# Input layer norm of a streaming encoder layer: mean, centring, then squares, with half 1 centred between half 0's chunks

## What is computed

```python
def _layer_norm(x, g, b):
    xf = x.astype(jnp.float32)
    mu = jnp.mean(xf, axis=-1, keepdims=True)
    var = jnp.mean(jnp.square(xf - mu), axis=-1, keepdims=True)
    return ((xf - mu) * lax.rsqrt(var + LN_EPS) * g + b).astype(x.dtype)

hp = _layer_norm(jnp.concatenate([meta_rows, x_prompt], axis=1), ln_in_g, ln_in_b)
hs = _layer_norm(x_sample, ln_in_g, ln_in_b)
z = h @ w_in + b_in           # u, q, k, v and two gates, 1024 -> 4096
...                           # pooling mixer, stick-breaking attention, out projection, norm, MLP, norm
```

## Time and profile before

| | |
|---|---|
| median of 3 runs | 827.62 us (827.31 to 828.57) |
| the profiled execution, its own time | 829.96 us |
| its span | 828.2 us |
| mean granted TensorE clock | 0.988 |
| PE busy | 798.3 us, 96% of the span |
| DVE, ACT, POOL busy | 504.2, 390.8, 113.8 us |
| chain that ended last | PE 93%, DVE 5%, ACT 1% |
| HBM traffic | 71 MB, mean 85 GB/s |

### The profile page before, as it was taken

The page is one execution under the profiler, slowest core; times in us unless marked ns, Lnnn a source line. Parts: engine busy times, 40 slices in busy tenths (PEclk is TensorE's granted clock), DMA queues, the critical chain, the costliest instruction groups (busy, mean ns, idle before and its releaser), DMA issues.

```text
span 828.2 us, 14458 instructions
## 1 busy us (share of the span) xinstructions
PE 798.3 (96%) x5859; PEld 766.6 (93%) x5859; DVE 504.2 (61%) x844; ACT 390.8 (47%) x653; POOL 113.8 (14%) x134
## 2 busy tenths in 40 slices
PE   4899999999999999999999999999999999999994
PEld 2789879998988899999999999999999999999994
DVE  6753434546454456885868678774767877445454
ACT  4542425655555465563546664333554433344333
POOL 5230000190000000006550000000000000000452
PEclk9799999999999999999999999999999999999997
DMA  9503222112111202234111214222221422222202
GB/s 352 200 28 135 77 96 75 56 39 80 53 51 51 75 28 77 78 103 151 51 53 52 70 57 153 77 103 77 77 70 57 154 77 102 77 77 84 70 29 86
DMA packets 23082, 71.62 MB, mean 86 GB/s; under 512 B 2464, under 2 KB 6704, under 8 KB 22640
## 3 DMA queue, kind: packets, MB, share of 16 engines
q1 hardware_dynamic: 22192, 67.97, 24.5%
q0 software_dynamic: 544, 2.52, 0.9%
q10 hardware_dynamic: 288, 0.33, 0.1%
HBM read 65.96 MB, written 4.85 MB: 85 GB/s over the span
## 4 chain that ended last, share of the span: by engine, by line
PE 93%; DVE 5%; ACT 1%; DMA 0%; issue 0%; POOL 0%; ACTq 0%; DVEq 0%
PE lin L582 14%; PE lin L583 14%; PE lin L584 14%; PE z L1018 5%; PE z L1021 5%; PE z L1020 5%; PE lin L923 3%; PE lin L924 3%; PE lin L925 3%; PE z L797 3%; PE lin L1064 2%; PE lin L1063 2%; PE lin L1062 2%; PE z L783 1%; PE z L855 1%; PE z L584 1%
## 5 line engine op out<-in xcount | busy, mean ns | idle before, releaser
L582 PE MATMUL lin<-h_hi,whi 128*128 128x288 f32 (+1 forms) x832 | 247.2, 297 | 0.0
L583 PE MATMUL lin<-h_lo,whi 128*128 128x288 f32 (+1 forms) x832 | 245.9, 296 | 0.0
L584 PE MATMUL lin<-h_hi,wlo 128*128 128x288 f32 (+1 forms) x832 | 245.0, 294 | 0.0
L584 PEld LDWEIGHTS lin<-h_hi,wlo 128*128 128x128 f32 x832 | 156.6, 188 | 0.0
L582 PEld LDWEIGHTS lin<-h_hi,whi 128*128 128x128 f32 x832 | 156.5, 188 | 0.1
L583 PEld LDWEIGHTS lin<-h_lo,whi 128*128 128x128 f32 x832 | 156.4, 188 | 0.1
L1706 DVE TENSOR_TENSOR wlo<-raw,whi 128x1024 fp32r<-128x1024 f32 x65 | 80.9, 1245 | 34.9 <-ACT whi L1095 29.8
L1095 ACT ACTIVATE whi<-raw 128x1024 fp32r<-128x1024 f32 x58 | 60.9, 1051 | 51.1 <-PE lin L584 32.8
L1512 ACT ACTIVATE relu_t<-lin,vecs 128x288 f32<-128x288 f32 x60 | 30.0, 500 | 91.5 <-PE lin L584 88.1
L2133 DVE TENSOR_TENSOR relu_sq<-relu_t 128x288 f32<-128x288 f32 x60 | 27.5, 458 | 64.7 <-ACT relu_t L1512 64.7
L1018 PE MATMUL z<-f_ops,whi 128*128 128x288 f32 x216 | 64.2, 297 | 0.7 <-issue 0.7
(11 more groups left out here) (332 smaller groups left out, 1908.9 us busy)
## 6 DMA issues: line engine op xcount, KB each, us to landing
raw<-w_stream SPq DMA_DIRECT2D x88, 512.0 KB, 3.5
w_set<-w_sets SPq DMA_DIRECT2D x32, 384.0 KB, 3.6
r<-x_t SPq DMA_DIRECT2D x8, 296.0 KB, 5.6
y<-r SPq DMA_DIRECT2D x16, 144.0 KB, 1.9
kcache<-k_cache SPq DMA_DIRECT2D x1, 2048.0 KB, 13.9
vcache<-v_cache SPq DMA_DIRECT2D x1, 2048.0 KB, 10.5
k_new<-k_t POOLq DMA_DIRECT2D x1, 1184.0 KB, 4.8
v_new<-v_t POOLq DMA_DIRECT2D x1, 1024.0 KB, 5.7
```

Of the source, the lines that this page charges most:

```text
L582: pe.matmul(out, w_h, hi, start=first, stop=False)
L583: pe.matmul(out, w_h, lo, start=False, stop=False)
L584: return pe.matmul(out, w_l, hi, start=False, stop=last)
```

## The change

The norm takes another order. Of half 0, DVE adds the raw chunks by pairs and PE sums them: the mean comes first, with no shift. DVE centres six chunks and POOL two (BY_DVE0 = (6, 8)), ACT squares six of the centred chunks and DVE two, whose sum is added, and PE sums the seven squares. The variance stays in its PSUM bank: ACT's Ln reads it there, with epsilon as bias, and DVE's Newton step starts from it there.

Of half 1, PE sums the eight raw chunks directly as the mean, ahead of the keys. Its chunks are centred on DVE between half 0's scale and low part, squared on ACT between half 0's high parts, and summed by PE between the chunks of the first pair of key units (`between`).

PE begins with 14 products of the constant matrix by itself (WARM), 128 columns each, into a bank that nobody reads. The low part of key unit 0 goes from POOL to DVE. On SP, units 0 and 1 go ahead of x's half 1, units (1,0) and (1,1) ahead of `bv` and the key cache, the value cache behind units (1,2) and (1,3), and `wpool` last, from ACT's queue. POOL makes its mask constants directly after unit 1's low part, and waits for half 1's Ln before it fills `mask_new`, whose place holds epsilon until then.

The diff, cut to its core:

```diff
-        BY_DVE0 = (5, 4)
+        BY_DVE0 = (6, 8)
+        SQ_ACT0 = (0, 1, 2, 6, 3, 4)
+        SQ_DVE0 = (5, 7)
+        WARM = 14
...
-            for j in range(RAW):
-                load_unit(0, j, first=True)
+                for j in range(2 * h, 2 * h + 2):
+                    load_unit(0, j, first=True)
+            load_unit(1, 0)
+            load_unit(1, 1)
             sp.dma_start(bv[:, :], bv_d).then_inc(bv_in, 16)
             sp.dma_start(kcache[:, :, :], kc_d).then_inc(kc_in, 16)
-            load_unit(1, 0)
-            load_unit(1, 1)
-            sp.dma_start(vcache[:, :, :], vc_d).then_inc(vc_in, 16)
             load_unit(1, 2)
             load_unit(1, 3)
+            sp.dma_start(vcache[:, :, :], vc_d).then_inc(vc_in, 16)
+            sp.dma_start(wpool[:, :, :], wpool_d).then_inc(wpool_in, 16)
...
-            def x_shift(h):
-                pe.wait_ge(x_in[h][0], 16)
-                pe.matmul(r0_shift(h), ones_f[:, :], r0[:, 0, half0(h)], start=True, stop=True).then_inc(n0_shift, 1)
-            def pair_sums(h, p):
-                c, start, stop = half0(h), p == 0, p == KC // 2 - 1
-                pe.wait_ge(pair_added, h * (KC // 2) + p + 1)
-                pe.matmul(r0_mean(h), inv_d[:, :], pair0[:, p, c], start=start, stop=stop)
-                pe.wait_ge(pair_sq_added, h * (KC // 2) + p + 1)
-                pe.matmul(r0_sq(h), inv_d[:, :], sq0[:, sq0_slot(2 * p), c], start=start, stop=stop)\
-                    .then_inc(n0_terms, 1)
-            pe.wait_ge(made, 2)
-            x_shift(0)
-            pair_sums(0, 0)
-            x_shift(1)
-            for p in range(1, KC // 2):
-                pair_sums(0, p)
+            def warm():
+                pe.matmul(lin[:, 1, 0:P], inv_d[:, :], inv_d[:, :], start=True, stop=True)
+            def square_sum(h, slot, first, last):
+                op = pe.matmul(r0_sq(h), inv_d[:, :], sq0[:, slot, half0(h)], start=first, stop=last)
+                if last:
+                    op.then_inc(n0_terms, 1)
+            pe.wait_ge(made, 1)
+            for _ in range(WARM):
+                warm()
+            for p in range(KC // 2):
+                pe.wait_ge(pair_added, p + 1)
+                op = pe.matmul(r0_mean(0), inv_d[:, :], pair0[:, p, :], start=p == 0, stop=p == KC // 2 - 1)
+            op.then_inc(n0_summed, 1)
+            for n, k in enumerate(SQ_ACT0):
+                pe.wait_ge(n0_sq, n + 1)
+                square_sum(0, k, n == 0, False)
+            pe.wait_ge(n0_sq_v, 3)
+            square_sum(0, SQ_DVE0[0], False, True)
+            for k in range(KC):
+                pe.wait_ge(x_in[1][k // 2], 16)
+                op = pe.matmul(r0_mean(1), inv_d[:, :], r0[:, k, half0(1)], start=k == 0, stop=k == KC - 1)
+            op.then_inc(n0_summed, 1)
...
+                    if between is not None and 1 <= k <= KC:
+                        between(k - 1)
+            def square_sum1(k):
+                pe.wait_ge(n0_sq, len(SQ_ACT0) + k + 1)
+                square_sum(1, k, k == 0, k == KC - 1)
+            keys_pair(0, 0, square_sum1)
...
-                act.wait_ge(n0_d, KC * h + k + 1)
-                if k >= 6:
-                    act.wait_ge(n0_terms, h * (KC // 2) + 1)
-                elif h and k < 2:
-                    act.wait_ge(n0_terms, KC // 2)
-                nc.scalar.activation(sq0[:, sq0_slot(k), half0(h)], r0[:, k, half0(h)], ACT.Square).then_inc(n0_sq, 1)
-            def mean0_out(h):
-                act.wait_ge(n0_terms, (h + 1) * (KC // 2))
-                nc.scalar.activation(var0[:, half0(h)], r0_mean(h), ACT.Square).then_inc(n0_msq, 1)
-                nc.scalar.activation(mean0[:, half0(h)], r0_mean(h), ACT.Copy).then_inc(n0_mean, 1)
+                centred0(k, h)
+                nc.scalar.activation(sq0[:, k, half0(h)], r0[:, k, half0(h)], ACT.Square).then_inc(n0_sq, 1)
...
-                act.wait_ge(n0_var, 2 * h + 2)
-                nc.scalar.activation(rstd0[:, c], var0[:, c], ACT.Ln).then_inc(n0_guess, 1)
+                act.wait_ge(n0_terms, h + 1)
+                nc.scalar.activation(rstd0[:, c], r0_sq(h), ACT.Ln, bias=eps0[:, :]).then_inc(n0_guess, 1)
...
+            act.wait_ge(n0_summed, 1)
+            nc.scalar.activation(mean0[:, :], r0_mean(0), ACT.Copy).then_inc(n0_mean, 1)
+            for k in SQ_ACT0:
                 square0(k, 0)
             split_keys(0)
             split_keys(1)
+            act.wait_ge(made, 2)
             root0(0)
             act.wait_ge(vecs_in, 16)
             norm0_hi(0, 0)
+            for k in range(1, KC):
+                norm0_hi(k, 0)
+                square0(k - 1, 1)
+                if k in (4, 6):
+                    split_keys(k // 2)
+            square0(7, 1)
...
+            def add_pair(p):
+                dve.wait_ge(x_in[0][p], 16)
+                tt(pair0[:, p, :], r0[:, 2 * p, half0(0)], r0[:, 2 * p + 1, half0(0)], ALU.add).then_inc(pair_added, 1)
+            def centre0(k, h):
                 if k == 0:
+                    dve.wait_ge(n0_summed, h + 1)
+                if k == 0 and h == 0:
+                    dve.wait_ge(n0_mean, 1)
+                tt(r0[:, k, half0(h)], r0[:, k, half0(h)], r0_mean(h), ALU.subtract).then_inc(n0_centred_v, 1)
+            def squares_0():
+                a, b = SQ_DVE0
+                dve.wait_ge(n0_centred_v, BY_DVE0[0])
+                tt(sq0[:, a, half0(0)], r0[:, a, half0(0)], r0[:, a, half0(0)], ALU.mult).then_inc(n0_sq_v, 1)
+                dve.wait_ge(n0_centred_g, KC - BY_DVE0[0])
+                tt(sq0[:, b, half0(0)], r0[:, b, half0(0)], r0[:, b, half0(0)], ALU.mult).then_inc(n0_sq_v, 1)
+                dve.wait_ge(n0_sq_v, 2)
+                tt(sq0[:, a, half0(0)], sq0[:, a, half0(0)], sq0[:, b, half0(0)], ALU.add).then_inc(n0_sq_v, 1)
             def inverse0(h):
+                c, out = half0(h), r0_rstd(h)
+                dve.wait_ge(n0_guess, 3 * h + 1)
+                nc.vector.tensor_scalar(out, r0_sq(h), LN_EPS, -0.5, ALU.add, ALU.mult).then_inc(n0_rstd, 1)
                 dve.wait_ge(n0_guess, 3 * h + 3)
+                dve.wait_ge(n0_rstd, 3 * h + 1)
+                tt(out, out, guess0[:, c], ALU.mult).then_inc(n0_rstd, 1)
+                dve.wait_ge(n0_rstd, 3 * h + 2)
+                stt(out=out, in0=out, scalar=1.5, in1=rstd0[:, c], op0=ALU.add, op1=ALU.mult).then_inc(n0_rstd, 1)
+                dve.wait_ge(n0_rstd, 3 * h + 3)
...
+                dve.wait_ge(*square_taken0(k, h))
...
+                add_pair(p)
+            for k in range(BY_DVE0[0]):
+                centre0(k, 0)
+            squares_0()
+            split_keys(0)
             inverse0(0)
             dve.wait_ge(vecs_in, 16)
             scale0(0, 0)
+            for k in range(1, KC):
                 scale0(k, 0)
+                centre0(k - 1, 1)
+                norm0_lo(k - 1, 0)
+            centre0(7, 1)
...
+            pool.wait_ge(n0_mean, 1)
+            for k in range(BY_DVE0[0], KC):
+                nc.gpsimd.tensor_tensor(r0[:, k, half0(0)], r0[:, k, half0(0)], mean0[:, :], ALU.subtract)\
+                    .then_inc(n0_centred_g, 1)
+            pool.wait_ge(lo_split, 1)
             lo_part(1)
...
+            pool.wait_ge(n0_guess, 4)
             nc.gpsimd.memset(mask_new[:, :, :], 0.0).then_inc(win_done, 1)
```

More of the change, by code:

```diff
@@ L709, in keys_pair @@
                         last = keys_half(m0 + 1, h, k - LAG)
-                last.then_inc(done, 1)
-            keys_pair(0, 0)
-            for p in range(KC // 2):
-                pair_sums(1, p)
+                        if k == KC + LAG - 1:
+                            last.then_inc(done, 1)
+                    if between is not None and 1 <= k <= KC:
[4 more added lines that the diff above has]
+            keys_pair(0, 0, square_sum1)
             keys_pair(2, 0)
@@ L1210, in key_out @@
                                      bias=vec(V_BIN + C_K + m)).then_inc(bank_free[m % 2], 1)
-            for k in range(KC):
+            act.wait_ge(n0_summed, 1)
+            nc.scalar.activation(mean0[:, :], r0_mean(0), ACT.Copy).then_inc(n0_mean, 1)
+            for k in SQ_ACT0:
                 square0(k, 0)
@@ L1215, in _ @@
             split_keys(1)
-            mean0_out(0)
-            for k in range(3):
-                square0(k, 1)
+            act.wait_ge(made, 2)
             root0(0)
@@ L1799, in add_pair_sq @@
-            def add_pair_sq(p, h):
-                c, slot = half0(h), sq0_slot(2 * p)
-                dve.wait_ge(n0_sq, KC * h + 2 * p + 2)
-                tt(sq0[:, slot, c], sq0[:, slot, c], sq0[:, slot + 1, c], ALU.add).then_inc(pair_sq_added, 1)
-            def variance0(h):
-                c = half0(h)
-                dve.wait_ge(n0_msq, h + 1)
-                stt(out=var0[:, c], in0=r0_sq(h), scalar=LN_EPS, in1=var0[:, c], op0=ALU.add, op1=ALU.subtract)\
-                    .then_inc(n0_var, 1)
-                dve.wait_ge(n0_var, 2 * h + 1)
```

(29 more changed lines are left out.)

92 lines of the change are left out of this document (20 added, 72 removed).

## The result

| | before | after |
|---|---|---|
| median | 828.1 us (827.31 to 829.78, 4 runs) | 820.9 us (820.67 to 821.17, 4 runs) |
| profiled execution | 829.96 us | 820.9 us |
| its span | 828.2 us | 819.1 us |
| mean granted clock | 0.988 | 0.996 |

The ratio of after to before is 0.9908, with an interval of [0.9896, 0.992]: 7.6 us faster by the ratio (7.2 by the two medians), where 9.1 had been forecast. It was counted down from the 827.62 us of the three runs at hand; the four runs of this comparison have 828.1.

A forecast was written before the change was run, and what follows sets the result against it. TensorE was taken as nearly always busy, so only an earlier or fuller start of its queue could pay. Terms 4.5 + 2.0 + 2.7 = 9.2, taken as 9.1, against the 827.62 us median gave 818.5 us; range 816.8 to 822.3.

The forecast's parts named there:

- first key product: End of half 0's norm: PE's first key product at 19.15 us against 23.7, a gain of 4.5.
- first pair and half 1's sums: Half 0's first pair of key units with half 1's square sums: 12.35 us against 14.4, a gain of 2.0.
- the rest of the keys: Half 0's second pair unchanged at 6.5 us; half 1's first pair 6.75 against 9.4, a gain of 2.7.
- Loads and mean: Front of half 0: fourth x piece at 7.1 us, mean at 9.2, seven squares summed at 0.50 each by 14.15.
- Constants: Fourteen constant products at PE's start: 0.43 us each, 6.0 in all, ending at 7.1 with the clock then full.
- The rival in which they don't lift the clock: Constants leave PE's clock at half until 13.5 us: everything 1.9 later, 820.4 us; chance 0.12.
- POOL holds DVE: DVE's PSUM step waits for POOL's split until 17.0: 820.0 us, or 821.6 with an h_lo held too; chance 0.12.
- The new wait: DVE's first h_lo stands behind half 1's first centring, which waits for half 1's mean until 18.15 us.
- Chunks: Half 0's chunks: DVE takes 1.24 us each, last h_lo at 28.0, pair and half 1's square sums end at 31.5.
- Half 1: Half 1's first pair: 6.75 us against 9.4, h_lo ending at 42.1 because ACT's high parts queue behind key outputs.
- Elsewhere: Behind the keys: later cache and wpool loads and POOL's moved mask part cost nothing.
- Slower: PE's clock stays at half throughout the front, the whole gain is lost: 829.7 us; chance 0.04.

The follow-up runs named there:

- before_look: The kernel before, unchanged, run again for a second profile of its front: 829.03 us.
- after_lo_first: The changed kernel with each h_lo of half 0 ahead of the centring of half 1's chunk: 820.39 us, ratio 0.99 to the kernel before.
- after_three: The changed kernel with h_lo ahead of half 1's centring, the old load order, and two ACT high parts ahead of key outputs: 819.63 us, ratio 0.9892.
- after_pool_pairs: The changed kernel with half 1's squares added by pairs on POOL, so PE sums four instead of eight: 822.93 us, ratio 0.9933.
- after_sums_behind: The changed kernel with half 1's eight square sums behind the first pair of key units instead of between its chunks: 824.62 us, ratio 0.9962.

## Why the prediction was right, and where its size was off

The mechanism came as forecast: an earlier first key product, a first pair that hides half 1's sums, and a first pair of half 1 that is fed, each within 0.5 us of its term against the profile that the prediction read. The range held as well. That the profiled execution's span came out as 819.1, forecast and measured, is in part luck: the keys' end gave 8.5 of the 9.1 us, and 0.6 lie behind the keys, where nothing was forecast and no part explains them. The terms, against the two profiles of the kernel before:

| term | forecast | against the profile read | against before_look |
|---|---|---|---|
| first key product | 4.5 | 23.71 - 19.73 = 4.0 | 21.92 - 19.73 = 2.2 |
| first pair and half 1's sums | 2.0 | 14.11 - 12.39 = 1.7 | 15.03 - 12.39 = 2.6 |
| the rest of the keys | 2.7 | 22.70 - 19.90 = 2.8 | 22.65 - 19.90 = 2.8 |
| sum | 9.2, taken as 9.1 | 8.5 | 7.6 |

The right column's sum equals the gain by the ratio, but the spans of its two profiles differ by 8.2 us, 0.6 of them again behind the keys; two profiles don't fix it closer than that.

**The step that was mis-sized** is the last: "It was 2.34 above the median of the runs, 827.62; against that I forecast **818.5 us**." It takes the whole 9.1 us, read from an execution of 829.96, off the median, as if that execution's excess stood on both sides. It didn't: the execution after had none (820.9, its median 820.9). Of the 2.4 us between forecast and measurement, 0.5 lie in the base (827.62 of three runs, 828.1 of four). L1812's long form accounts for at most 0.9: "Gain 4.5" counted 1.8 of it as removed, but between the two profiles of the old kernel only 0.92 reached the keys' end. With that priced, the forecast would have been 819.4 (827.62 less 9.1 - 0.9). The other 1.0 stays open. How many executions have the long form isn't known: one of four profiles of the old order with the variance in SBUF shows it, and its runs spread from 826.68 to 830.08 us.

By its own steps:
- **Loads and mean.** The fourth x piece was there at 8.0, not 7.1; the mean ended at 9.35 (forecast 9.2) and the square sums took 0.54 each instead of 0.50. From there all is some 0.5 late: squares summed 14.65 (forecast 14.15), half 1's mean 18.65 (18.15), first product 19.73 (19.15).
- **Constants.** 6.09 us for fourteen, 6.0 forecast. They ran at the half-level price that the sum gave them, and behind them the sums were at full level, as said. But the square sums were at full level without them too. The rival in which they don't lift the clock, with a rise at 13.5 us as before, was wrong in the same way: without any constants the square sums were at full level from 10.8.
- **POOL holds DVE.** It didn't: 0.47 us at 15.30 in the middle of POOL's split (14.89 to 17.25). The Trainium skill ("SBUF — State Buffer", SBUF: two separate sides) has whichever starts first of a GpSimd operation and a DVE one in a two-port mode or with two SBUF inputs (the latter against a GpSimd operation that reads SBUF) keep the other out for its whole length. This step, PSUM to PSUM, came out free as that page gives, and the trace agrees for L1812, long and short, and for the h_lo and Newton steps of the old order, which ended 0.17 us (L1812) and 0.32 to 0.33 us (the others) behind POOL's instruction. The prediction saw this in L1812 alone. It priced the new Newton steps at 0.5 us each, which is right, but didn't say that the old ones, 0.75 and 0.96, were held too, nor that POOL's additions for half 1 slowed the first pair.
- **The new wait.** Half 1's mean did stand ahead of the first h_lo, and nothing worse. Moving it behind (after_lo_first) gained 0.5 by the medians, 0.7 by the ratios, neither clear of nothing.
- **Chunks.** DVE's pace of 1.24 us and the last h_lo at 27.85 (28.0) held, and the pair with its sums took 12.39 (12.35). After 32.1 came the second pair in 6.51.
- **Half 1.** 6.86 (6.75), with the last h_lo at 42.8 (42.1), for the reason given, which after_three confirms by removing it (6.53).
- **Elsewhere.** Nothing was taken back; the rest of the span was 0.6 us shorter, which no part explains and other kernels of the same order spread over as well.
- **Slower.** The clock was at full level from the mean's sums to the end of the keys in the profiled execution; only the constants ran at the half-level price (0.43 us each), though the clock column says 1.00 there. That it can fall, behind a PE as thin as 0.52 to 0.60 busy, several experiments show, but none of them lost the 9.1 us that this rival needs.

What carries the gain, by taking out one part at a time: the interleaving of the halves 6.0 us against the one late place tried, the square sums between the chunks 3.7, of which 2.3 are placed (the two overlap: the sums can stand there only because the centring does), the variance in its bank 1.6 in the old order, constants and loads nothing that can be measured. The mean taken first, with its shares of DVE and POOL, was not taken out by itself.

## What to carry to other kernels

Price an edit against what an ordinary execution holds: an operation that takes five times its usual length in the one profile at hand may hang on which of two engines started a quarter of a microsecond earlier, so take a second look before a gain is built on it, and don't subtract such a gain from a median. Where DVE operations on SBUF are longer than their like, hold their ends against the ends of POOL's instructions. Work that delays the first half may pay where it makes the second half ready, if the delay is small change by chunk (0.37 us) and the wait that it removes is whole. Before small work is taken off PE, look at what else keeps it busy there: in after_pool_pairs the clock fell and the time rose.

## What the runs showed of the hardware

- The clock fell to half level behind stretches in which PE was busy 2.70 of 5.20, 2.90 of 4.83 and 2.58 of 4.30 us, with no single wait above 1.3 us; it held behind 3.62 of 4.27 and 7.95 of 9.42.
- Half 0's square sums, seven behind a gap of 1.5 us, took 3.75 us in most profiles and 5.45 in two (after_sums_behind, after_lo_first), with the clock at 0.69. The code ahead of them is the same. What decides is open.
- A DVE operation with all its tensor inputs in SBUF that started under a split, an addition or a centring of POOL never ended before it, up to the keys' end in all thirteen profiles, and the short ones ended a fixed time behind it: the tensor_scalar L1812 0.17 us behind it (2.27 us long in one execution, 0.48 in another of the same kernel, 0.84 in half 1), 128 x 296 operations with two inputs in SBUF 0.32 to 0.33 us behind it (h_lo at 1.07 us, Newton steps at 0.75, 0.96 and 1.10). The centrings and Newton steps with an input in PSUM kept their 0.45 to 0.47 us beside POOL's splits.
- The same holds for the additions that after_pool_pairs gave to POOL, but there it costs little, because h_lo met them late:

```profile
20.38 0.81 POOL L2452 TENSOR_TENSOR sq<-sq 128x296 f32<-128x296 f32 x1 [2.27 <-ACT sq L1190]
...
20.92 0.60 DVE L1850 SCALAR_TENSOR_TENSOR h_lo<-r,vecs,h_hi 128x296 fp32r<-128x296 f32 x1
```

Three h_lo of the first pair took 0.60 us there, the others 0.52, as all do in the kernel after.
